# Where the operands of split fp32r matmuls begin: high parts at 192 of 256 bytes, low parts at 64, in place of both at 64

## What is computed

```python
def first_block(x, ...):                      # two layers
    for i in range(2):
        mix = dsa_mixer(h, ...) if i == 0 else gla_mixer(h, ...)
        h = layer_norm(DN_ALPHA * h + mix, ...)
        h = layer_norm(DN_ALPHA * h + jnp.square(jax.nn.relu(h @ w_up)) @ w_down, ...)   # width 4096
...
def second_block(x, mem, ...):                # one layer
    h = _rms_norm(x, norm_mix_pre)
    (a_q, a_k, a_v, f_q, f_k, f_v, f_g, c_u, s_x, s_b, s_c) = jnp.split(h @ w_in, cuts, axis=-1)
    ...                                       # four branches ya, yf, yc, ys of width 512
    proj = jnp.einsum('bsnc,ncd->bsnd', br, w_branch)
    gates = jax.nn.sigmoid(h @ w_gate + b_gate).reshape(B, S, N_BRANCH, D)
    x = x + _rms_norm(jnp.sum(gates * proj, axis=2) @ w_out, norm_mix_post)
    ...                                       # attention over mem: w_xq, w_xkv, w_xo
    u = _dwconv_causal(_rms_norm(x, norm_ffn_pre) @ w_up, ffn_dw) + ffn_dw_b
    x = x + _rms_norm((jax.nn.silu(u_g) * u_v) @ w_down, norm_ffn_post)                 # width 2816
```

## The kernel before

| tensor | role | before |
|---|---|---|
| whi, wlo (49,280 and 82,048 on) | weights | 128 |
| xh (131,392), xl (139,584) | activations | 64, 64 |
| fh (170,560), fl (186,944) | activations | 64, 64 |
| gh (170,560), gl (193,088) | activations | 64, 64 |
| bhi (214,208), blo (218,304) | activations of the branches | 192, 192 |
| mhi, mlo (from 170,688 on) | activations of mem | 192, 192 |

## Time and profile before

### The profile page before, as it was taken

One profiled execution on the slowest core, in us unless ns is written; L12 is line 12 of the kernel. 1 busy time (PEld: TensorE's weight loads), 2 busy tenths in 40 slices (PEclk: granted clock), 3 DMA queues, 4 the chain that ended last, 5 costly groups with the idle time before them and its releaser, 6 DMA issues.

```text
span 1257.2 us, 24535 instructions
## 1 busy us (share of the span) xinstructions
PE 1222.2 (97%) x10378; PEld 1184.8 (94%) x10378; DVE 872.9 (69%) x1382; ACT 670.4 (53%) x876; POOL 39.4 (3%) x30
## 2 busy tenths in 40 slices
PE   9989999999999999999999999999999999999997
PEld 8868999999988999999999999989999999999997
DVE  6867865566747687645676534879988667899843
ACT  6445453353456434534535548675465576777741
POOL 0431000000000000000000001000000000000000
PEclk9999899999999899999999999999999999999999
DMA  9213255455339242564552559965445432555430
GB/s 362 99 68 137 99 199 203 167 190 187 132 137 262 80 151 108 180 222 169 208 193 73 201 176 276 282 199 199 154 162 202 172 126 97 206 184 184 167 135 34
DMA packets 30666, 213.11 MB, mean 170 GB/s; under 512 B 3680, under 2 KB 4192, under 8 KB 5232
## 3 DMA queue, kind: packets, MB, share of 16 engines
q1 hardware_dynamic: 27792, 195.83, 42.9%
q0 software_dynamic: 2016, 14.68, 5.8%
q10 hardware_dynamic: 768, 1.31, 0.3%
HBM read 210.76 MB, written 1.05 MB: 168 GB/s over the span
## 4 chain that ended last, share of the span: by engine, by line
PE 52%; DVE 5%; ACT 3%; issue 3%; ACTq 0%; DVEq 0%
PE lin L514 15%; PE lin L516 15%; PE lin L515 15%; ACT whi L1253 2%; PE att L650 1%; PE lin L657 1%; DVE wlo L1810 1%; PE lin L694 1%; PE lin L544 1%; PE lin L551 1%; DVE z L1920 1%; PE lin L545 0%; DVE sqr L2148 0%; PE att L730 0%; PE att L769 0%
## 5 line engine op out<-in xcount | busy, mean ns | idle before, releaser
L1810 DVE TENSOR_TENSOR wlo<-raw,whi 128x2048 fp32r<-128x2048 f32 x165 | 377.2, 2290 | 173.1 <-ACT whi L1253 172.0
L514 PE MATMUL lin<-xh,whi 128*128 128x256 f32 x1712 | 482.0, 282 | 2.6 <-DVE amax L2095 1.1
L515 PE MATMUL lin<-xl,whi 128*128 128x256 f32 x1712 | 478.0, 279 | 0.0
L516 PE MATMUL lin<-xh,wlo 128*128 128x256 f32 x1712 | 477.9, 279 | 0.0
L1253 ACT ACTIVATE whi<-raw 128x2048 fp32r<-128x2048 f32 x183 | 348.9, 1909 | 155.0 <-PE lin L516 140.6
L514 PEld LDWEIGHTS lin<-xh,whi 128*128 128x128 f32 x1712 | 322.8, 189 | 5.6 <-issue 3.8
L515 PEld LDWEIGHTS lin<-xl,whi 128*128 128x128 f32 x1712 | 324.8, 190 | 0.6 <-issue 0.5
L516 PEld LDWEIGHTS lin<-xh,wlo 128*128 128x128 f32 x1712 | 322.8, 189 | 0.0
L514 PE MATMUL lin<-fh,whi 128*128 128x256 f32 x512 | 143.4, 280 | 1.6 <-DVE fl L2151 1.6
L516 PE MATMUL lin<-fh,wlo 128*128 128x256 f32 x512 | 142.9, 279 | 0.0
L515 PE MATMUL lin<-fl,whi 128*128 128x256 f32 x512 | 142.9, 279 | 0.0
(11 more groups left out here) (396 smaller groups left out, 1928.5 us busy)
## 6 DMA issues: line engine op xcount, KB each, us to landing
raw<-units_dram SPq DMA_DIRECT2D x183, 1024.0 KB, 4.8
wlo<-units_dram POOLq DMA_DIRECT2D x14, 1024.0 KB, 13.4
h<-x_dram SPq DMA_DIRECT2D x1, 1024.0 KB, 6.8
out_dram<-h SPq DMA_DIRECT2D x4, 256.0 KB, 2.0
consts<-consts_dram SPq DMA_DIRECT2D x1, 864.0 KB, 15.8
narrow_a<-narrow_a_dram SPq DMA_DIRECT2D x1, 544.0 KB, 9.0
aqT<-mem_dram ACTq DMA_DIRECT2D x1, 512.0 KB, 6.3
fkT<-mem_dram ACTq DMA_DIRECT2D x1, 512.0 KB, 7.4
```

Of the source, the lines that this page charges most:

```text
L514: mm(out, w[0], a[0], start=first, stop=False)
L515: mm(out, w[0], a[1], start=False, stop=False)
L516: return mm(out, w[1], a[0], start=False, stop=last)
L1810: v.tensor_tensor(wlo[u % RING][:], raw[u % RING][:], whi[u % RING][:].bitcast(f32), ALU.subtract).then_inc(lo_ready, 1)
```

## The change

The fillers are cut and moved, so that 128 bytes that stood ahead of a high part stand between it and the low part. xh, fh and gh begin 128 bytes lower, at 192 of 256 (131,264, 170,432 and 170,432). xl, fl, gl and every tensor behind them stay where they were, and the instructions and their order are the same.

```diff
-        sbuf("ahead_of_x", [P, 48])
+        sbuf("ahead_of_x", [P, 16])
         xh = sbuf("xh", [P, DB, S], f32r)
+        sbuf("between_x", [P, 32])
         xl = sbuf("xl", [P, DB, S], f32r)
...
-        _, fh, fl, relu0, relu1, sqr0, sqr1 = stage(
-            ("ahead_of_f", [P, 32]), ("fh", [P, 16, S], f32r), ("fl", [P, 16, S], f32r), ("relu0", [P, 2, S]), ("relu1", [P, 2, S]),
+        fh, _, fl, relu0, relu1, sqr0, sqr1 = stage(
+            ("fh", [P, 16, S], f32r), ("between_f", [P, 32]), ("fl", [P, 16, S], f32r), ("relu0", [P, 2, S]), ("relu1", [P, 2, S]),
             ("sqr0", [P, 2, S]), ("sqr1", [P, 2, S]))
...
-        _, gh, gl, fpad0, fpad1, fconv, fth, fy = stage(
-            ("ahead_of_g", [P, 32]), ("gh", [P, FB, S], f32r), ("gl", [P, FB, S], f32r), ("fpad0", [P, 2, 2 + S]), ("fpad1", [P, 2, 2 + S]),
+        gh, _, gl, fpad0, fpad1, fconv, fth, fy = stage(
+            ("gh", [P, FB, S], f32r), ("between_g", [P, 32]), ("gl", [P, FB, S], f32r), ("fpad0", [P, 2, 2 + S]), ("fpad1", [P, 2, 2 + S]),
```

## The result

The changed kernel takes 1269.87 us (median of four runs, 1268.8 to 1271.24) against 1252.22 of the kernel before (four runs, 1248.91 to 1253.47). That is 1.013 times the time before, interval 1.0095 to 1.0164: 1.3% slower, +17.6 us between the medians. Put beside the kernel before a second time, it was 1267.83 against 1251.18, a ratio of 1.0141 (1.0107 to 1.0175). The profiled execution took 1269.06 us, 10.1 us more than that of before.

A forecast was written before the change was run, and what follows sets the result against it. PE's matmul stream, busy 97%, was taken as the bound. Close stretches +11.6, wide ones -1.7 and pairs of high parts +0.7 us gave +10.6, say +11: 1251.9 + 11 = 1263 us (1270 profiled), range 1248 to 1272.

The forecast's parts named there:

- token products: 144 products of three matmuls with xh and xl as weights; taken as nothing, 1 us either way.
- The high parts: Moving operands in two of three matmuls per triple: 117.8 ns whatever the pace before, +4.3 ns each in close stretches.
- close triples: About 1,000 three-matmul products of x, f and g in stretches at 113.5 ns per matmul; predicted +11.6 us together.
- close pace: The shorter of two steady start-to-start distances in PE's stream, 113.5 ns per matmul, against 117.7 to 117.9 for the wide one.
- The low parts: One matmul in three, behind a high part: 116.5 ns, +3.0 in a close stretch, -1.2 in a wide one.
- a distance beyond 118 in a full stream: Sign that the prediction is wrong: matmuls more than 118 ns apart anywhere in a full stream.
- wide stretches: Nine stretches of PE's stream at about 117.8 ns per matmul, 1,400 triples; predicted to give back 1.7 us.
- upper bound: Sum if low parts stay at 117.8 ns: 1,000 x 12.9 ns + 0.7 us = +13.6 us.
- The alternation helps: Rival: differing places in successive matmuls break the wide pace, giving back 18 us, 1234 us; chance 0.17.
- No measurable change: Rival: within 0.3% (3.8 us), if low parts return to 113.5 ns at once or the start makes no difference; chance 0.17.
- More than 117.8: Rival: high parts beside wide-pace neighbours cost more; 2 ns more on each would be 10 us, 1273; chance 0.03.
- f and g might be spared: Case where fh and gh, at 448 of 512 bytes, pay nothing: about 2 us less loss.

The follow-up runs named there:

- both_192: Kernel before with high and low parts of x, f and g all beginning at 192 of 256 bytes; 1268.92 against 1257.41 us, ratio 1.0103.
- low_192: Kernel before with the low parts of x, f and g at 192 and the high ones at 64; 1268.6 against 1257.41 us, ratio 1.0091.
- x_only: Kernel before with only xh moved to 192, f and g left at 64; 1260.07 against 1257.41 us, ratio 1.0024.
- primed: Kernel before plus three matmuls reading at 160 of 256 bytes at 11 places; 1250.22 against 1254.41 us, ratio 0.9977; second time ratio 1.0007.
- fg_only: Kernel before with only fh and gh moved to 192, xh left at 64; 1259.16 against 1254.41 us, ratio 1.0028.
- 320/320 and 448/448: Streams of triples without the network, high/low parts both at 320 or both at 448 of 512 bytes, weights at 128; 117.8 ns each on both visits.
- streams by themselves: Kernels without the network, running only streams of such matmuls at varied operand places; no ratio, 113.3 to 121.2 ns per matmul.
- three stream kernels: Three kernels without the network: one varies operand places, one the matmuls ahead of a stream, one further places and matmuls inserted mid-stream; profiled once each, no ratio.

## Where the prediction held and where it did not

**The direction and the bound held.** The time is that of PE's stream; no other engine and no wait took part. +11 us were forecast, 1270 for a profiled execution (it was 1269.06) and 1263 for the median (it was 1269.87, inside the range, 7 us above the point). That 1270 came so near is in part luck: the high and low parts cost 2.5 us more than the sum had, and the token products and the breaks gave 3 us back, for which it had nothing.

**The high parts.** "117.8 ns, whatever the pace before them", +4.3 ns each in 1,000 close triples (950 by the distances): the close pace of the high parts went as forecast, their 2052 close distances became 99, but they cost 12.8 us in place of the 9.3 in the sum. As a mechanism it was wrong. `both_192` runs 1118 matmuls at 113.3 ns with everything at 192, and `low_192` loses as much with half as many matmuls at 192. What keeps the changed kernel from the close pace is that two places alternate in a triple, which has no close pattern in 16 visits; a stream at 192 alone would have come to nearly the same loss, since it seldom enters the close one. I had 4 branches and 480 matmuls at 192 for a rule on the place, and they were few independent entries into a stream.

**The low parts** (116.5 ns: +3.0 in a close stretch, -1.2 in a wide one): their own distance was right (116.4 for x), and the step that failed is the next one, to take the high part beside it as unchanged. It costs 118.0 to 119.6, and a triple is at 353.3 ns. The text had named a distance beyond 118 in a full stream as a sign of being wrong, and here it is. The -1.7 us of the wide stretches did not come, and a close triple lost 13.2 ns (353.3 - 340.1), not the 11.6 of the sum. That puts the sum near the upper bound (+13.6); measured are +13.1 over high and low parts.

**The token products**, taken at nothing with 1 us either way, gave back 1.1 us: 433 of 497 distances are close, before 196 of 502. This is of the kind that `x_only` showed: a plain stream behind an alternating one. In both traces of the changed kernel it was so.

**From 10 to 17.6 us.** The forecast for the median rested on the share of close pace in one trace, and named the weak point: were the 7 us between the profiled execution of before and its median a different share, the loss would be larger by as much. Profiled against unprofiled, us:

| kernel | profiled | median of the runs beside it |
|---|---|---|
| before | 1258.96; 1261.5 | 1252.22; 1257.07 (one run) |
| after | 1269.06; 1265.95 | 1269.87; 1267.83 |
| primed | 1250.86; 1248.95 | 1250.22; 1251.56 |

Of these three only the kernel before has its profiled executions above the others, by 4 to 7 us; the two kernels whose pace is settled, one wide, one close, don't show it. The two traces of before are two draws, and within the spread of its runs (1245.65 to 1262.35 us in all). Still, that fits an unprofiled kernel before with more close pace than its traces: 6.7 us at 4.4 ns are 1,500 matmuls, some 4,600 in all, and then priming (some 6,000) would gain 1,400 x 4.4 = 6 us less 33 x 0.118 = 4 us for its own matmuls, -2 us in all; -4 and +0.4 were measured. The clock, which is on record for every run, bears it out. At 0.993 and 0.994 seven runs of before took 1246.37 to 1258.98 us and four of `primed` beside them 1247.83 to 1250.19; beside the second `primed` it was seven runs, 1245.65 to 1254.88, and three, 1245.92 to 1248.95. So before still draws where primed doesn't, but 8 of those 14 draws are no longer than 1249.1, as short as the primed ones. Priming takes away the long runs and hardly moves the rest. The pace itself of an execution without a profile stays unseen, and so this is support, not proof. The text had both numbers, 1263 and 1270, and took the lower.

**The rivals.** "The alternation helps", 17%, was the wrong way round. Its argument, that the wide pace at 64 can't hold where neighbours differ, holds only for plain streams that stand behind an alternating one. "No measurable change" fell with both ratios. "More than 117.8": single high parts do reach 119.6 ns, but not the triple. That f and g might be spared by lying at 448 of 512 is refuted by the changed kernel's trace, by `fg_only`, and by 320/320 and 448/448, which read as 64 wide and as 192.

The Trainium skill (TensorE: Matmul & The Clock Gate, part 2, step by step) has two independent read ports, one for the moving operand and one for the weights. The prediction read it so that no start has a price. The streams by themselves disagree with that reading, with 113.3 to 121.2 ns at one clock and no other work. The same page's N/2.4 + 2.5 ns (back-to-back issue gap), which it gives for a matmul in isolation and not for a stream with a weight load each, is an estimate of 109.2 ns for 256 columns; no stream that ran reached it, and the nearest is 113.3.

**What stays open.** What picks the pace at the start of a stream. It isn't the number of fp32 matmuls ahead (3, 4, 5 and 7 of them precede close and wide visits alike) or the output bank, and a kind of stream that was close in 7 of 8 visits was wide in the eighth. Nor is it known why three matmuls at 160 settle it, or why full streams at another place lead to the close pace and short ones don't.

## What to carry to other kernels

Where PE is busy 97% with fp32r matmuls of 256 columns and a weight load each, look at the distance from start to start, not at the duration, and keep all moving operands of a stream at one place of 256 bytes, 64 below the weights (here 64 and 128): mixing two places, even for one matmul in three, cost 1%, and so did 64 above them for all. Compare times at equal granted clock, which goes with 5 us and more between runs of one kernel. Before a price is put on a place, count how often the stream was entered anew, not how many matmuls it holds; and take the map of such paces from more than one trace, since it differs between executions of the same program.

## What the runs showed of the hardware

- The distance of 256-column fp32r matmuls with a new weight block each, at 2.4 GHz, depends on the start of the moving operand less that of the weights, modulo 256 bytes: 120.0 ns at 0, 118.7 at 128, 116.7 at 16 and 32, 113.3 or 117.8 at 64 and at -64 (113.3 seen only with weights at 128), 121.2 for triples with high parts at -128 and low ones at -64. Mixed placements fit the rule less well: 448/64 is at 117.0, 192/64 at 117.8 or 117.0.
- At 64 away there are two steady paces, for the same kind of entry, the same number of fp32 matmuls ahead and the same output bank. One is picked within the first half dozen matmuls of a stream and kept over 1,100 matmuls and more, until a break or an operand at another place.
- Three matmuls that begin 32 bytes above their weights set the close pace in 16 of 16 visits, also in the middle of a wide stream, and at 22 of 22 entries in the whole kernel.
- In the network without primers, x at 64 behind a full stream at 192 (bhi, blo) takes the close pace in 9 of 9 cases, with primers elsewhere in 6 of 6.
- In the three stream kernels, the first fp32r matmul behind an fp32 one is 198 to 207 ns from its successor, at every place.
